# A hybrid encoder layer: gate/up pairs of both FFNs by seven block products, four token quarters, and x kept in DRAM between sub-layers

## The chip, the cores and the metric

One core of one Trainium2 chip runs the whole kernel as one launch. The time is device microseconds of that core, the median of three runs. Five engines work side by side: TensorE (PE, with its weight loads listed apart as PEld), VectorE (DVE), ScalarE (ACT), GpSimd (POOL), and SyncE (SP), which issues most DMAs. Matrix products land in eight PSUM banks; DVE and ACT read them out.

## The reference, cut to what matters

1024 prompt tokens and 32 sample tokens go together through one layer, so every product has 1056 token columns. d_model is 1024 (8 tiles of 128), d_ff 2816 (22 tiles).

```
x += 0.5 * post(SwiGLU_1(pre(x)))            # w_gu 1024x5632, w_down 2816x1024
h = pre(x); z = h @ W_in                     # 8 heads of q|f|i|og, pooling input, gates
yA = up_A(gnorm(HGRN2(q,f,i)) * silu(og));   yB = up_B(pooled mix)
x += post(W_out(sigmoid(gA)*yA + sigmoid(gB)*yB))
x += 0.5 * post(SwiGLU_2(pre(x)))
x += post(sigmoid(pre(x) @ W_pg) * (p @ W_pp))
swiglu(h) = (silu(h @ w_gate) * (h @ w_up)) @ w_down      # pre, post: RMSNorm with gains
```

## The kernel before, in words

Features lie on partitions, tokens on the free axis. The 1056 tokens are G = 3 groups of N = 352. The precision is kept by splitting both operands into two float16 parts, so each 128x128 weight tile costs three matmuls per group (lines 524 to 526: high weight by high x, high weight by low x, low weight by high x).

Weights stream in as units of four tiles (128x512 float32, 256 KB). SP loads a unit into a ring of 11 slots once PE has finished with the slot (line 423). POOL then makes the two float16 parts with three operations: times 32 into `wtmp` (471), high part (473), low part (475), and counts `unit_ready`.

Nothing reorders work at run time: each engine has its own program written by hand, and semaphores tie them. `STAGES` lists the stages: `units` per turn, `turns`, `ks` (how many weight tiles each output column sums over) and `banks`. A turn makes the output tiles (t, g) in order "M" (all groups of column t, then the next), "G" (all columns of group g, then the next) or "P" (pairs), and tile number `pos` of a turn goes to PSUM bank `pos % banks`. PE may start a tile only when the bank's last content was read (`take`, `bank_read`). Every unit of a turn keeps its slot in the next turn, so a turn's units are reloaded as PE leaves them.

- `ffn*_up` computes 44 gate and up columns, 11 turns of 4 columns. ACT applies Silu to a gate tile from PSUM (785), DVE multiplies the up tile in (1170) and splits the product into `hid` (1173, 1174).
- `ffn*_down` sums 22 tiles per column, 2 columns a turn, the last turn in order G. ACT squares (803) and copies (811) each output tile.
- Between sub-layers, per group: `post` scales and adds into x (1133, 1135), `pre` sums squares (1092, 1095), scales (1105) and splits h (1112). These are DVE's; ACT squares (766) and makes the high part (775).
- `heads`: eight turns in which PE computes the next head's four columns and, hooked in between tiles, the pieces of the last head's recurrence (605, 618, 633, 638, 649). DVE frees the q and og tiles by finishing their Silu (1203, 1197).
- `gates`: per output column m, two gate columns (ACT, 984), then the two up-projections, whose tiles DVE multiplies (1409) and joins with three SBUF operations (1415 to 1417).
- `ple`: gate and embedding columns, 2 turns in order G.

Of the kernel before, what the change touches and what calls it, by code (L numbers as in the profile page):

```python
# [13 lines left out]
P = 128  # L22
# [9 lines left out]
G = 3  # L32
N = T // G
C = 64
# [4 lines left out]
UT = 4  # L39
PARTS, PART = 4, KD // 4  # L40

# [5 lines left out]
    "ffn1_up": dict(units=8, turns=11, ks=[KD] * 4, kinds="G" + "P" * 10, banks=6),  # L47
    "ffn1_down": dict(units=11, turns=4, ks=[KF] * 2, kinds="MMMG", banks=6),
    "head0": dict(units=8, turns=1, ks=[KD] * 4, kinds="G", banks=6),
    "heads": dict(units=8, turns=HEADS, ks=[KD] * 4, kinds="M" * HEADS, banks=4),  # L50

    "gates0": dict(units=8, turns=1, ks=[KD, KD, 1, 1, 1, 1, KD, 4], kinds="M", banks=6),
    "gates": dict(units=7, turns=7, ks=[KD, KD, KD, 4], kinds="M" * 7, banks=6),
    "out0": dict(units=6, turns=1, ks=[KD] * 3, kinds="M", banks=3),
    "out1": dict(units=10, turns=1, ks=[KD] * 5, kinds="G", banks=5),
    "ffn2_up": dict(units=8, turns=11, ks=[KD] * 4, kinds="G" + "P" * 10, banks=6),
    "ffn2_down": dict(units=11, turns=4, ks=[KF] * 2, kinds="MMMG", banks=6),
    "ple": dict(units=10, turns=2, ks=[KD, KP] * 4, kinds="GG", banks=6),
}
ORDER = list(STAGES)  # L60
RING = max(s["units"] for s in STAGES.values())
# [12 lines left out]
CALLS += [("post", 3, g) for g in range(G)]  # L74
Y_STAGES = [["ffn1_down"], ["out0", "out1"], ["ffn2_down"], ["ple"]]

# [23 lines left out]

NEXT_UP, NEXT_PLE = 2, 3
# [5 lines left out]


# [11 lines left out]
EARLY = [1, 2, 1]  # L120
# [9 lines left out]
def jobs_of(name, kind):  # L130

    a = len(STAGES[name]["ks"])
    if kind == "M":
        return [(t, g) for t in range(a) for g in range(G)]
    if kind == "G":
        return [(t, g) for g in range(G) for t in range(a)]
    return [(2 * q + r, g) for q in range(a // 2) for g in range(G) for r in range(2)]


class Plan:  # L140


    def __init__(self):
        uses = [0] * 8
        unit = 0
        loads = [0] * RING
        first = 0
        self.base, self.unit0, self.load0, self.first, self.used0 = {}, {}, {}, {}, {}
        used = 0
        self.hg_base = None  # L150
        self.norm = []
        norm_uses = iter(range(len(CALLS)))

        def norms(k):
            for _ in range(k):
                c = next(norm_uses)
                b = 6 + c % 2
                self.norm.append((b, uses[b]))
                uses[b] += 1

        before = {"ffn1_up": 3, "head0": 6, "ffn2_up": 6, "ple": 6}
        for name in ORDER:
# [3 lines left out]
            self.unit0[name] = unit  # L166
# [1434 lines left out]
```

## Time and profile before

| | us |
|---|---|
| median of 3 runs (lowest, highest) | 2683.82 (2682.93, 2685.84) |
| span of the profiled execution | 2682.0 |
| PE busy / PEld busy | 2512.2 / 1654.7 |
| DVE / ACT / POOL busy | 1139.9 / 468.1 / 1528.6 |

The profiled execution's span lies 1.8 us below the median of the runs. PE's busy time is modelled: a matmul is listed at about 0.31 us, while two that follow each other start closer together than that, so the busy share says only where PE stood still. How far a stage is from PE's pace is read from a window's length and its count of matmuls. POOL's idle time before line 471 is nearly all a wait for a weight load, which in turn waits for PE to leave the slot.

### The profile page before, as it was taken

What the parts mean: (1) busy time and instruction counts of PE and PEld (TensorE: products, weight loads), DVE (VectorE), ACT (ScalarE), POOL (GpSimd) and SP (SyncE); (2) the same over time, 40 slices, a digit from 0 to 9 for tenths busy, and PEclk for the clock granted to TensorE, in tenths of its full rate; (3) what the DMA queues carried; (4) which work ended last, traced back from release to release, by engine and by line L of the source; (5) the groups of instructions that cost most, each with busy time, mean ns of one, the idle gap of its engine ahead of it and who ended that gap; (6) DMA issues with size and microseconds to landing.
All of it is one profiled execution on the core that took longest, in us unless ns stands there. A gap on an engine that the chain in (4) does not pass through costs nothing.

```text
span 2682.0 us, 43535 instructions
## 1 busy us (share of the span) xinstructions
PE 2512.2 (94%) x17172; PEld 1654.7 (62%) x17172; DVE 1139.9 (43%) x1526; ACT 468.1 (17%) x782; POOL 1528.6 (57%) x1293
## 2 busy tenths in 40 slices
PE   5999999999979898989899999979999999999797
PEld 3666666666646666666565666646666666666454
DVE  7322222100386677767773233285222222010854
ACT  3000000000222222222220000132000000001243
POOL 4765566766375545454643667744666657565531
PEclk9999999999989999999999999999999999999999
DMA  2211111121011111111110111101111112111111
GB/s 101 64 47 47 47 51 54 52 59 44 24 44 37 35 34 34 34 34 34 47 35 28 44 54 63 44 28 48 47 47 47 47 47 63 56 44 44 56 40 65
DMA packets 74973, 125.28 MB, mean 47 GB/s; under 512 B 9744, under 2 KB 19984, under 8 KB 74896
## 3 DMA queue, kind: packets, MB, share of 16 engines
q1 hardware_dynamic: 66096, 118.26, 14.7%
q10 hardware_dynamic: 8800, 5.94, 0.7%
q8 instruction: 55, 0.90, 0.1%
q14 instruction: 22, 0.18, 0.0%
HBM read 118.73 MB, written 5.44 MB: 46 GB/s over the span
## 4 chain that ended last, share of the span: by engine, by line
PE 77%; DVE 18%; issue 3%; POOL 1%; ACT 1%; DMA 0%; DVEq 0%; POOLq 0%; ACTq 0%
PE bank L524 24%; PE bank L525 24%; PE bank L526 24%; DVE hid L1276 3%; DVE scratch L1105 2%; DVE x L1135 1%; DVE hy L1133 1%; DVE hid L1250 1%; DVE u L1092 1%; DVE part_sum L1092 1%; PE bank L638 1%; DVE hy L1112 1%; PE bank L547 1%; PE bank L618 1%; PE bank L605 1%
## 5 line engine op out<-in xcount | busy, mean ns | idle before, releaser
L524 PE MATMUL bank<-hy,ring 128*128 128x352 f16 x3552 | 1123.9, 316 | 26.2 <-DVE hy L1112 12.5
L525 PE MATMUL bank<-hy,ring 128*128 128x352 f16 x3552 | 1122.4, 316 | 0.0
L526 PE MATMUL bank<-hy,ring 128*128 128x352 f16 x3552 | 1121.5, 316 | 0.0
L471 POOL TENSOR_TENSOR wtmp<-ring,wconst 128x512 f32<-128x512 f32 x429 | 482.6, 1125 | 1032.7 <-DMA ring<-weights 1004.3
L475 POOL TENSOR_TENSOR ring<-wtmp,ring 128x512 f16<-128x512 f32 x429 | 539.8, 1258 | 33.7
L473 POOL TENSOR_TENSOR ring<-wtmp,wconst 128x512 f16<-128x512 f32 x429 | 505.8, 1179 | 33.6
L524 PE MATMUL bank<-hid,ring 128*128 128x352 f16 x1593 | 501.3, 315 | 7.7 <-DVE hid L1397 6.0
L525 PE MATMUL bank<-hid,ring 128*128 128x352 f16 x1593 | 500.9, 314 | 0.0
L526 PE MATMUL bank<-hid,ring 128*128 128x352 f16 x1593 | 500.6, 314 | 0.0
L524 PEld LDWEIGHTS bank<-hy,ring 128*128 128x128 f16 x3552 | 352.1, 99 | 220.3 <-DVE hy L1112 15.9
L526 PEld LDWEIGHTS bank<-hy,ring 128*128 128x128 f16 x3552 | 351.3, 99 | 189.0
L525 PEld LDWEIGHTS bank<-hy,ring 128*128 128x128 f16 x3552 | 351.2, 99 | 186.6 <-issue 3.2
L1170 DVE SCALAR_TENSOR_TENSOR pair_buf<-bank,pair_buf 128x352 f32<-128x352 f32 x132 | 69.2, 524 | 615.2 <-PE bank L526 613.7
L1127 DVE TENSOR_TENSOR u<-u,pair_buf 128x352 f32<-128x352 f32 x84 | 64.8, 771 | 411.3 <-ACT pair_buf L803 410.7
L524 PEld LDWEIGHTS bank<-hid,ring 128*128 128x128 f16 x1593 | 156.9, 98 | 92.8 <-DVE hid L1397 6.4
L525 PEld LDWEIGHTS bank<-hid,ring 128*128 128x128 f16 x1593 | 156.9, 98 | 85.9 <-issue 3.6
L526 PEld LDWEIGHTS bank<-hid,ring 128*128 128x128 f16 x1593 | 156.8, 98 | 83.3
L785 ACT ACTIVATE pair_buf<-bank 128x352 f32<-128x352 f32 x132 | 60.7, 463 | 822.5 <-PE bank L526 822.5
L1174 DVE TENSOR_TENSOR hid<-pair_buf,hid 128x352 f32 (+1 forms) x132 | 124.5, 943 | 17.5
L1409 DVE SCALAR_TENSOR_TENSOR hid<-bank,hid 128x352 f32<-128x352 f32 x48 | 24.9, 519 | 188.1 <-PE bank L526 188.1
L547 PE MATMUL bank<-u,cst 128*128 128x352 f32 x48 | 27.4, 663 | 71.8 <-DVE u L1095 47.1
L1276 DVE TENSOR_TENSOR hid<-hid 128x1088 f32<-128x1088 f32 (+1 forms) x64 | 91.0, 1488 | 0.0
(127 smaller groups left out, 1505.8 us busy)
## 6 DMA issues: line engine op xcount, KB each, us to landing
ring<-weights SPq DMA_DIRECT2D x429, 256.0 KB, 2.6
out_x<-x SPq DMA_DIRECT2D x12, 352.0 KB, 2.3
x<-xT ACTq DMA_DIRECT2D x4, 704.0 KB, 5.9
x<-xT SPq DMA_DIRECT2D x2, 704.0 KB, 5.2
hid<-pT ACTq DMA_DIRECT2D x1, 1056.0 KB, 5.3
out_states<-scratch ACTq DMA_DIRECT2D x16, 64.0 KB, 2.4
scratch<-state_in ACTq DMA_DIRECT2D x8, 64.0 KB, 1.8
cst<-consts ACTq DMA_DIRECT2D x1, 128.0 KB, 5.2
```

Of the source, the lines that this page charges most:

```text
L471: chain.inc(nc.gpsimd.tensor_tensor(wtmp[:], raw, ws_all, ALU.mult))
L473: chain.inc(nc.gpsimd.tensor_tensor(hi, wtmp[:], one_all, ALU.mult))
L475: done.inc(nc.gpsimd.tensor_tensor(lo, wtmp[:], hi, ALU.subtract))
L524: nc.tensor.matmul(out, whi, rhs(t, k, g, 0), start=(k == 0), stop=False)
L525: nc.tensor.matmul(out, whi, rhs(t, k, g, 1), start=False, stop=False)
L526: mm = nc.tensor.matmul(out, wlo, rhs(t, k, g, 0), start=False, stop=end)
L547: nc.tensor.matmul(bank[b][:, 0:N], ones, ssq(g), start=True, stop=True).then_inc(bank_full[b], 1)
L785: nc.scalar.activation(pair_buf[:, n % 2, :], bank[b][:, 0:N], ACT.Silu, scale=1.0 / WS)\
L1127: V_.tensor_tensor(ssq(g), ssq(g), pair_buf[:, n % 2, :], ALU.add).then_inc(ysq_added, 1)
L1170: V_.scalar_tensor_tensor(out=s, in0=bank[b][:, 0:N], scalar=1.0 / WS, in1=s, op0=ALU.mult, op1=ALU.mult).then_inc(bank_read[b], 1)
L1174: V_.tensor_tensor(dst[:, N:2 * N], s, dst[:, 0:N], ALU.subtract).then_inc(hidden_ready, 1)
L1276: V_.tensor_tensor(out, out, in0, ALU.mult).then_inc(operand_ready, 1)
```

## The change

Groups: G = 4, N = 264. PSUM banks per stage: 7 for tiles (banks 0 to 6) and bank 7 for the norms' sums, where 6 and 2 stood (heads keep 4). The ring has 16 slots.

Gate and up tiles j are computed as one 2x2 block product: the two output columns by the two halves of the 8 k-tiles (weight blocks a, b, c, d of one unit each), times the two halves of h by two token quarters. Seven products (Winograd's form, with the u sums taken after PSUM) of 4 k-tiles replace eight. Columns 0 and 1 of gate and up are still computed directly (`up0`, one turn of 4 columns), then 20 pairs follow. The sums of h (T1 to T4) are made once per FFN, before the pairs; those of the weights once per pair.

```diff
-G = 3
+G = 4
+RING = 16
+BANKS = 7
-    "ffn1_up": dict(units=8, turns=11, ks=[KD] * 4, kinds="G" + "P" * 10, banks=6),
-    "ffn1_down": dict(units=11, turns=4, ks=[KF] * 2, kinds="MMMG", banks=6),
+    "ffn1_up0": dict(units=8, turns=1, ks=[KD] * 4, kinds="G", banks=BANKS),
+    "ffn1_up": dict(pairs=KF - 2),
+    "ffn1_down": dict(units=11, turns=4, ks=[KF] * 2, kinds="MMMG", banks=BANKS),
...
-    "gates": dict(units=7, turns=7, ks=[KD, KD, KD, 4], kinds="M" * 7, banks=6),
+    "gates": dict(units=7, turns=7, ks=[KD, KD, KD, 4], kinds="M" * 7, banks=BANKS),
...
+PRODUCTS = 7
+OPERAND = (0, 2, 3, 4, 1, 5, 6)
+PAIR_BANKS = ((0, 1), (2, 3), (6, 7), (4, 5), (0, 1), (4, 5), (2, 3))
...
+            def pair(name, p):
+                pool.wait_ge(scaled, p * RAWS + (sums + 4))
...
+                summed(wtmp[:], c, d, ALU.add)
+                pool.wait_ge(wsum_ready, p * RAWS + (sums + 1))
+                summed(f, wtmp[:], a, ALU.subtract)
+                lo(0)
+                pool.wait_ge(wsum_ready, p * RAWS + (sums + 2))
+                lo(1)
+                summed(c, a, c, ALU.subtract)
+                pool.wait_ge(wsum_ready, p * RAWS + (sums + 3))
+                lo(2)
+                lo(3)
+                lo(4)
+                pool.wait_ge(unit_ready, p * PRODUCTS + (plan.ready0[name] + 2))
+                summed(f, b, f, ALU.subtract)
+                pool.wait_ge(wsum_ready, p * RAWS + (sums + 4))
+                lo(5)
+                lo(6)
...
+            def pair(name, p, ready=None):
+                for k in range(PRODUCTS):
+                    for e in range(2):
...
+                        take(b, uses)
+                        for kk in range(KH):
...
+                with act.Fori(0, STAGES[name]["pairs"] - 1) as i:
+                    scale(name, i + 1)
+                    to_high(name, i + 1, range(5), product_before(i))
+                    silu_pair(f, i, 0)
+                    to_high(name, i + 1, [5], product_before(i))
+                    silu_pair(f, i, 1)
+                    to_high(name, i + 1, [6], product_before(i))
...
-                    V_.tensor_tensor(xg(g)[:, ks, :], xg(g)[:, ks, :], y[:, ks, :], ALU.add).then_inc(x_updated, 1)
+                    V_.tensor_tensor(xq(min(q + 1, 3), g)[:, ks, :], xq(min(q + 1, 3), g)[:, ks, :], y[:, ks, :], ALU.add).then_inc(x_updated, 1)
```

So POOL does 11 operations per pair (4 sums, `summed`, and 7 low parts, `lo`) where 12 stood for the same four units; the scaling and the high parts go to ACT (11 operations of 128x512). The weight parts of product k are single: they are remade once product k of the pair before is done. DVE adds each of a pair's 14 PSUM tiles to running sums (`tile`, 128x264 from PSUM), and at the end of a pair does per half a multiplication, a high part and a low part of 128x528. x is no longer resident: ACT's queue stores each quarter to `out_x` after `post` and loads it back during the next down stage (8 stores and 12 loads of 1056 KB).

Four places where the order changed, each as it stands in the programs.

TensorE, the gates stage, from the last two tiles of a turn into the next turn. Before: `hid` as operand is an up-projection tile, `hy` a gate tile of the next turn.

```order
L524 MATMUL bank4<-hid,ring 128x352 [waits bank_read4]
...
L524 MATMUL bank5<-hid,ring 128x352 [waits bank_read5]
...
L518 ISA [waits bank_read0]
L524 MATMUL bank0<-hy,ring 128x352 [waits unit_ready]
...
L524 MATMUL bank1<-hy,ring 128x352 [waits bank_read1]
```

After, the same place:

```order
L714 MATMUL bank0<-hid,ring 128x264 [waits bank_read0]
...
L714 MATMUL bank1<-hid,ring 128x264 [waits bank_read1]
...
L708 ISA [waits bank_read0]
L714 MATMUL bank0<-ops,ring 128x264 [waits unit_ready]
...
L714 MATMUL bank1<-ops,ring 128x264 [waits bank_read1]
```

The first two tiles of a turn now use the banks of the last two tiles of the turn before; before, they used those of its first two up-projection tiles.

VectorE, between the last `pre` and the first pair of an FFN, after: L1507 to L1513 finish a direct tile, L1523 forms a T sum of h, L1533 its low part.

```order
L1507 SCALAR_TENSOR_TENSOR work<-bank4,work 128x264 [waits bank_full4,bank_read3]
...
L1523 TENSOR_TENSOR hid<-hid 128x4x264
L1523 TENSOR_TENSOR hid<-hid 128x4x264 [waits t_summed]
...
L1533 TENSOR_TENSOR ops<-hid,ops 128x4x264 [waits t_hi] x2
L1523 TENSOR_TENSOR hid<-hid 128x4x264 x2
L1507 SCALAR_TENSOR_TENSOR work<-bank6,work 128x264 [waits bank_full6,bank_read5]
...
L1507 SCALAR_TENSOR_TENSOR work<-bank1,work 128x264 [waits bank_full1,bank_read0]
...
L1533 TENSOR_TENSOR ops<-hid,ops 128x4x264 [waits t_hi] x4
```

The direct tiles in banks 0 and 1 are read behind six T sums and two low parts, and the first pair's first product needs those banks.

GpSimd, one pair, after (L636 is a sum, L632 a low part; the operations of before are the three of lines 471, 473 and 475, four times).

```order
L636 TENSOR_TENSOR ring<-wtmp,ring 128x512 [waits wsum_ready]
L627 REGISTER_ALU
L632 TENSOR_TENSOR ring<-ring 128x512 [waits whi_ready]
L653 REGISTER_ALU
L627 REGISTER_ALU [waits wsum_ready]
L632 TENSOR_TENSOR ring<-ring 128x512 [waits whi_ready]
L636 TENSOR_TENSOR ring<-ring 128x512
```

POOL now waits on ACT (`whi_ready`) ahead of each low part, where its three operations of a unit waited only on POOL itself.

## Rows read from the trace of the kernel before

**Rows 1.** Page: busy microseconds, share of the span, instructions.
```profile
PE 2512.2 (94%) x17172; PEld 1654.7 (62%) x17172; DVE 1139.9 (43%) x1526; ACT 468.1 (17%) x782; POOL 1528.6 (57%) x1293
```
**Rows 2.** Windows by stage: from:to length, busy (count) per engine, granted clock, DMA.
```profile
82.10:511.70 429.60, 429.60 (x2882) 281.80 (x2880) 112.36 (x180) 27.79 (x60) 282.72 (x256) 1.00 0.18 51
511.70:762.60 250.90, 242.41 (x1594) 157.52 (x1592) 56.29 (x52) 35.60 (x64) 141.50 (x125) 0.99 0.16 47
827.20:1382.50 555.30, 502.36 (x3986) 351.58 (x3985) 396.04 (x597) 152.47 (x219) 296.61 (x208) 0.96 0.12 35
1434.80:1697.90 263.10, 263.10 (x1766) 172.60 (x1764) 78.30 (x103) 18.80 (x42) 168.54 (x152) 1.00 0.17 52
```
**Rows 3.** Groups by line, weight loads: count, busy us, mean ns, idle before.
```profile
L524 PEld LDWEIGHTS bank<-hy,ring 128*128 128x128 f16 x3552 | 352.1, 99 | 220.3 <-DVE hy L1112 15.9 <-ACT hid L1018 6.3 <-POOL ring L475 5.6
```
**Rows 4.** Chain of waits in a head turn, 34 short f32 products: start, us.
```profile
931.24 2.24 PE bank L605 x68
```
**Rows 5.** Timeline, POOL in the gates stage: start, us, [idle before].
```profile
1446.89 1.04 POOL L471 TENSOR_TENSOR wtmp<-ring,wconst 128x512 f32<-128x512 f32 x1 [31.61 <-DMA ring<-weights]
1448.01 1.04 POOL L473 TENSOR_TENSOR ring<-wtmp,wconst 128x512 f16<-128x512 f32 x1
1449.13 1.15 POOL L475 TENSOR_TENSOR ring<-wtmp,ring 128x512 f16<-128x512 f32 x1
...
1472.96 1.20 POOL L473 TENSOR_TENSOR ring<-wtmp,wconst 128x512 f16<-128x512 f32 x1
1474.24 1.32 POOL L475 TENSOR_TENSOR ring<-wtmp,ring 128x512 f16<-128x512 f32 x1
```
**Rows 6.** Timeline, PE in the gates stage.
```profile
1443.61 0.31 PE L526 MATMUL bank<-hy,ring 128*128 128x352 f16 x1
...
1467.03 0.31 PE L524 MATMUL bank<-hid,ring 128*128 128x352 f16 x1
```
**Rows 7.** Timeline, DVE over the joins of that turn.
```profile
1469.09 0.52 DVE L1409 SCALAR_TENSOR_TENSOR hid<-bank,hid 128x352 f32<-128x352 f32 x1 [1.27 <-PE bank L526]
...
1473.18 0.51 DVE L1409 SCALAR_TENSOR_TENSOR hid<-bank,hid 128x352 f32<-128x352 f32 x1
...
1476.98 0.51 DVE L1409 SCALAR_TENSOR_TENSOR hid<-bank,hid 128x352 f32<-128x352 f32 x1
```
**Rows 8.** Groups by line and shape, ACT and DVE.
```profile
L1170 DVE SCALAR_TENSOR_TENSOR pair_buf<-bank,pair_buf 128x352 f32<-128x352 f32 x132 | 69.2, 524 | 615.2 <-PE bank L526 613.7 <-ACT pair_buf L785 1.5
L803 ACT ACTIVATE pair_buf<-bank 128x352 f32<-128x352 f32 x63 | 29.0, 460 | 330.1 <-PE bank L526 329.4 <-DVE u L1127 0.7
L811 ACT ACTIVATE hy<-bank,col 128x352 f32<-128x352 f32 x72 | 39.5, 549 | 0.0
L766 ACT ACTIVATE scratch<-x 128x1408 f32<-128x1408 f32 x24 | 32.7, 1375 | 64.5 <-DVE x L1135 59.4 <-issue 5.1
L1272 DVE TENSOR_TENSOR hid<-hid 128x1056 f32 x6 | 7.5, 1258 | 0.9
L1276 DVE TENSOR_TENSOR hid<-hid 128x1088 f32<-128x1088 f32 x32 | 53.4, 1707 | 0.0
```
**Rows 9.** The same view of POOL, 827.2 to 1382.5 us.
```profile
L473 POOL TENSOR_TENSOR ring<-wtmp,wconst 128x512 f16<-128x512 f32 x69 | 102.9, 1491 | 5.4
```
**Rows 10.** Timeline of a head turn, PE, state updates of the last head.
```profile
937.09 2.82 PE L618 MATMUL bank<-hid 64*128 64x128 f32 x32
942.18 0.48 PE L618 MATMUL bank<-hid 64*128 64x128 f32 x2
```
**Rows 11.** The same turn, DVE.
```profile
945.74 1.39 DVE L1203 SCALAR_TENSOR_TENSOR hid<-bank,hid 128x352 f32<-128x352 f32 x3
```
**Rows 12.** Timeline, DVE, last `pre` at the start.
```profile
50.63 2.63 DVE L1092 TENSOR_REDUCE u<-scratch 128x352 f32<-128x1408 f32 x1 [0.47 <-ACT scratch L766]
...
64.78 1.83 DVE L1112 TENSOR_TENSOR hy<-scratch,hy 128x704 f16<-128x704 f32 x2
```
**Rows 13.** Waits of PE, 2590 to 2640 us (`ple`): total, times, longest.
```profile
PE bank L524 <- POOL ring L475: 6.2, 4, 1.7
```

More of the change, by code:

```diff
@@ L181, in __init__, with per @@
                     uses[b] += HEADS * len(HG_PIECES) // 4
-        norms(3)
-        self.units = unit
+        norms(G)
+    def per(self, name, b):
+        s = STAGES[name]
+        return len(range(b, len(s["ks"]) * G, s["banks"]))
     def head_job(self, h, t, g):
@@ L443, in _ @@
                                      name == ORDER[0] and i == 0)
-                for u in range(s["units"]):
-                    last[plan.slot(name, u)] = plan.freed_by(name, s["turns"] - 1, u)
+                last.update(plan.slots_freed(name))
             for g in range(G):
@@ L477, in _ @@
             for name in ORDER:
                 s = STAGES[name]
-                first = 1 if name == ORDER[0] else 0
-                for i in range(first):
-                    for u in range(s["units"]):
-                        split(name, i, u)
-                if s["turns"] - first >= 3:
-                    with pool.Fori(first, s["turns"]) as i:
-                        chain.enter(i, first, 2 * s["units"])
-                        done.enter(i, first, s["units"])
+                if "pairs" in s:
+                    pair(name, 0)
+                    with pool.Fori(1, s["pairs"]) as p:
+                        pair(name, p)
+                    done.base += PRODUCTS * s["pairs"]
+                    continue
@@ L491, in _ @@
                 else:
-                    for i in range(first, s["turns"]):
+                    for i in range(s["turns"]):
                         for u in range(s["units"]):
@@ L1144, in add, with between @@
                         add_square(q, m, g)
+                def between(g):
+                    if g < G - 1:
+                        add(last[g + 1][:early[g + 1]])
+                    if q == 1 and g == 2:
+                        products(1, (0,))
+                    if q == 1 and g == G - 1:
+                        products(1, (2, 3))
+                    if q == 2 and g in (1, 2):
+                        split_p(g - 1)
+                    if q == 2 and g == G - 1:
+                        gated_products(range(NEXT_PLE))
@@ L1157, in products @@
-            def products(name, f, i, kind, ns):
-                pairs = [(pos, t, g) for pos, (t, g) in enumerate(jobs_of(name, kind)) if t % 2]
+                    add(last[g][early[g]:])
+                    if q == 1 and g == G - 1:
+                        products(1, (1,))
+                    c = post_call(q, g)
+                    post(q, c, g, yq(q, g))
+                    dve.wait_ge(x_updated, count_before(UPDATE_PARTS, q, g) + UPDATE_PARTS[q])
+                    pre(q + 1, c + 1, g, lambda: between(g))
```

700 lines of the change are left out of this document (505 added, 195 removed).

## The prediction

> **What bounds the kernel now.** I read the page first, then the windows by stage, then timelines. PE stands still for only 6% of the span [rows 1], and a window of gate/up columns shows why: 2880 f16 matmuls of 352 columns in 429.60 us, 149.2 ns each, at granted clock 1.00 (2.4 GHz) [rows 2]. 352 columns at 2.4 GHz are 146.7 ns, so 2.5 ns come on top. The gates run at the same pace, 1764 in 263.10 us. There PE alone sets the time, POOL is busy for 282.72 of 429.60 us and DVE for 112.36, and fewer columns are worth their full time. It is otherwise in the head turns: 2304 matmuls would need 343.7 us and the window is 555.30. In all, 15,444 f16 matmuls need 2304 of 2682.0 us; the other 378 are recurrence pieces, seams between sub-layers and the start. The question is which of PE's new bank and weight waits end last.
>
> **Matmuls.** At N = 264 a matmul should take 110 + 2.5 = 112.5 ns. Gate and up: before 2 x 3168 of 149.2 ns = 945.3 us. After, per FFN, 384 direct ones and 20 pairs x 7 x 2 x 4 x 3 = 3360; 7488 x 112.5 ns = 842.4 us. That is 103 us less. The other 9108 become 12,144, 1366 us for 1359: 7 us more. The weight load per matmul stays and has less to hide under: 99 ns [rows 3] against 112.5. I take no cost: in the heads, 68 short f32 products, each with its own load, pass in 2.24 us [rows 4], 33 ns each, so loads can follow each other closer than that.
>
> The Trainium skill (TensorE: Matmul & The Clock Gate, Back-to-back issue gap) gives for streams with a load per matmul about 131 ns at 512 columns and 81 ns at 128. The row of 149.2 ns at 352 already contradicts that curve and fits the page's other formula, N/2.4 + 2.5. By the curve's slope (0.13 ns a column) the 88 columns saved would give only 11.5 ns.
>
> **A pair, 18.9 us on PE (168 x 112.5 ns).** Who feeds it?
> - DVE: 14 tiles from PSUM. A PSUM read of 352 takes 524 ns also in the pair loop [rows 8]; less 88 columns at 0.96 per ns, 0.43 us each, 6.0. Then six SBUF operations of 528, 0.44 to 0.71 alone (1056 take 1.26 [rows 8]), at most 1.2 to 1.5 beside POOL. 14 us: under PE.
> - ACT: 1375 ns for 1408 and 460 for 352 [rows 8] give 0.60 us for 512, 13 operations, 8 us.
> - POOL: alone, 1.04, 1.04 and 1.15 us with gaps of 0.08 [rows 5]. A low part is as before, 1.15. A sum reads two full float32 tensors, not shown; between 1.04 and 1.2 I take 1.15, the nearest two-tensor row. 11 x 1.15 + 0.7 of gaps = 13.35. Two low parts start only after a sum and ACT's high part of it, 2 x 0.8 = 1.6. And each pair has a hole: block d may be reloaded only when the last low part is done, and the next pair's first sum needs it scaled. From PE's last use of a unit (1443.61 + 0.31 [rows 6]) to POOL's first operation on its successor (1446.89 [rows 5]) go 3.0 us; plus ACT's 0.6 and a semaphore, 3.7. Sum 18.65.
> - Contention: where DVE runs its joins, POOL's 1.04 becomes 1.20 and 1.15 becomes 1.32 [rows 5], behind DVE operations of 352. Those of 528 hold longer by 0.18 us, so about 0.35 each; three of the six should meet POOL: 1.05. Ends: 0 and, by POOL's 1.49 in the heads [rows 9] on all 11, 3.6. POOL's round is then 19.7 us (18.2 to 22.3), longer than PE's 18.9. POOL sets the pace.
>
> **Entry into the pairs.** Let t be the moment the last quarter of h is split. PE then has 8.8 us of direct tiles (3.25 of the quarter's four tiles at 2.7) and wants banks 0 and 1. Those hold the last two direct tiles, and DVE reaches bank 1 behind two finished tiles, six T sums and two T low parts (the order above). ACT scales four units (2.4), loads its Silu table (1.3), so DVE's two tiles end at t + 7.8; four T sums of 1.26 [rows 8] to 12.9; two low parts to 15.4; two sums beside POOL, 1.7 [rows 8], to 18.9; ACT's T high parts and one weight part (waiting for POOL's third sum) to 20.8, two Silus to 21.6, and bank 1 is free at 23.5. PE waits 13 us. The rest of pair 0 ends at t + 42, one POOL round after its last low part (t + 37.8) is too early for pair 1, whose first weights come at t + 37.8 + 3.7 + 3.6 = t + 45. The last pair ends at t + 45 + 18 x 19.7 + 18.9 = t + 418.5.
>
> t at the start is 66.5 now (end of the last low part [rows 12]). A group costs DVE 13.4 us alone (reductions 2.63 and 2.54, add 0.53, eight of 0.53, four of 0.88); a quarter 10.6. Four for three, one more norm wait (2), two more finished tiles in the chain (2.7), less 2 for the earlier first quarter: t = 71. FFN 1 then ends at 489.5, not 511.7: **-22**. FFN 2 counts from the end of its direct columns, t + 8.8; without the first FFN's sigmoid, 408.7 for 429.6: **-21**. Without POOL's pace and the entry this would be -52 each.
>
> **Down stages.** With POOL one round behind, it is done with the last pair 7 us before PE, two units' worth. The first tile wants six units in 7.4 us where POOL makes one in 3.46 [rows 5]: wait 7.5, some of it repaid in a slow clock, 9. Eight tiles on seven banks also put a turn's last tile and the next turn's first in bank 0: PE waits for ACT's square and copy (0.39 + 0.47 from 460 and 549 ns [rows 8], plus latency), 1.2 us x 3. In the last turn one quarter passes all 11 units in 14.9 us instead of 19.7, 2.4 more. 15 a stage: **+30**.
>
> **Head turns, +16.** The first f tile now uses the bank of the first q tile, which DVE frees after the state chain. In the row, updates start on PE at 937.09 [rows 10] and DVE's q multiplications at 945.74 [rows 11], first one done at 946.2: 9.1 us. PE's way from there to that f tile is now 2.8 (updates) + 0.5 + 33 matmuls (3.7), 7.0. The difference of 2.2 and latency, 2.3, seven turns. Before, that bank was free anyway.
>
> **Gates, +38.** The last up-projection tiles of a turn take PE 1.35 us each, and DVE joins one per 4.1 and 3.8 us (1469.09, 1473.18, 1476.98 [rows 7]): each of three SBUF operations waits for a POOL operation, so the smaller size saves little, 3.6. Counted from the first such matmul (1467.03 [rows 6]), the reads come at 1.6, 5.2, 8.8 and 12.4. The next turn's first gate tile needs bank 0, that is the third read: PE arrives at 5.4, gets it at 9.3, and the second tile waits from 12.0 to 12.9. 4.8 us x 7 = 33.6, and 4.4 for clock lost after such pauses. Were DVE alone, 2.0 a tile, it would be 0.7 x 7 = 5; with every pause slowing the clock, 46.
>
> **Seams and ends.** Quarters start the seam sooner (-4) and end it sooner (-3.5); DVE pays four sets of fixed costs (+5) and at the second seam two more tiles; I take -1 for three seams, bounds -20 and +25. `ple`'s second turn wants ten units in 13.5 us instead of 17.9; it waits 6.2 us for POOL now [rows 13], +8. The last post is shorter, -3. The DRAM copies of x are asked for a whole down stage ahead and stay hidden; uncovered, each would cost some 5 us, once per quarter.
>
> **Sum against the profiled span:** -22 - 21 + 30 + 16 + 38 - 1 + 8 - 3 + 7 = +52, minus 1 for what the stage sums already hold of the last 7 = +51: 2733, and with the 1.8 us to the median 2735.
>
> **Rivals.**
> 1. *DVE and POOL seldom meet* (faster). The six operations fall into POOL's hole, POOL's round is 18.2 and PE's 18.9 decides; the lead grows 0.7 per pair, so the down stages find their units. Each FFN -14 and -9, and joins at 2.0 a tile, -33: 2735 - 46 - 33 = 2656. It decides from contention under 0.25 us per pair. For it: the tail of a pair starts when POOL has 2 us left to do. Against: joins were slowed in every gates turn. 0.20.
> 2. *Only the bank waits fail to appear* in gates and heads, because DVE is earlier than I place it: 2735 - 54 = 2681, no change. Against: both orders are fixed. 0.09.
> 3. *POOL is slower:* a round of 21.5, as towards the heads' rows; 18 x 1.8 x 2 = +65: 2800. 0.14.
> 4. *Matmul spacing does not shrink with N:* the slope above gives 137.7 ns, 25.2 x 19,632 = +495. The pace of 33 ns [rows 4] speaks against it. 0.02.
>
> **Numbers.** Forecast 2735, chance 0.55, own range 2700 to 2770. For 8 in 10 the range goes to the first rival and most of the third: 2652 to 2795. A change under 0.2% (5.4 us) is what a measurement cannot tell from none. Faster 0.22 (rival 1 and a part of 2), same 0.05, slower 0.73.
>
> **What would show it.** A pair at 19 to 20 us between the starts of its first products, with PE waiting for POOL ahead of them; near 18.9 and no wait: rival 1. An idle PE of 13 us ahead of each first pair. 4 us ahead of the first gate tile of each gates turn, released by DVE's multiplication. 2 us ahead of the first f tile. Matmul starts 112 to 113 ns apart. The prediction is wrong if a pair takes under 18.9 or if those four waits sum to less than half of what is set down.

## The result, and the profile after

| | us |
|---|---|
| changed kernel, median of 4 runs (lowest, highest) | 2764.86 (2762.32, 2767.49) |
| kernel before, 4 runs beside it | 2684.11 (2682.93, 2685.84) |
| ratio, 95% interval | 1.0302 (1.0285 to 1.0318) |
| span of the profiled execution after | 2760.5 |

It became slower by 81 us, where +51 was forecast. The time lies inside the range, the sign is right, and the size is too small by 30 us. Both spans (2760.5 and 2682.0) differ by 78.5 us, and that difference can be laid out by stage from the start times of the matmuls:

| stretch | before | after | difference | forecast |
|---|---|---|---|---|
| start to the end of FFN1's pairs | 511.7 | 487.4 | -24.3 | -22 |
| `ffn1_down`, `head0` | 315.5 | 341.5 | +26 | +15 and a share of the seams' -1 |
| head turns | 555.3 | 594.1 | +39 | +16 |
| `gates0` | 52.3 | 43.8 | -8.5 | 0 |
| `gates`, `out0` | 295.3 | 338.6 | +43 | +38 |
| `out1` to the end of FFN2's pairs | 552.8 | 529.0 | -24 | -21 |
| `ffn2_down`, `ple`, tail | 399.0 | 426.2 | +27 | +15 and +5 |

The forecast column leaves out the +6 that its sum had for matmuls outside the FFNs (7, less 1), since no single stretch holds them. The profiled executions themselves scatter: in experiments that do not touch the heads, the head turns took 589 to 599 us, so a difference of a few microseconds in that row is not to be read.

The windows of after for the four stretches of [rows 2], same columns:

```profile
93.60:487.40 393.80, 384.46 (x3361) 328.69 (x3362) 254.36 (x407) 146.54 (x257) 285.62 (x224) 0.99 0.20 58
487.40:760.50 273.10, 245.39 (x2124) 208.96 (x2121) 74.15 (x80) 41.35 (x89) 168.57 (x150) 0.98 0.24 74
828.90:1423.00 594.10, 518.69 (x4755) 433.08 (x4753) 398.22 (x611) 157.31 (x251) 297.07 (x213) 0.93 0.12 34
1466.80:1770.20 303.40, 275.59 (x2354) 233.97 (x2351) 92.78 (x140) 21.85 (x56) 175.50 (x161) 0.96 0.18 50
```

The first is the pair stage alone (20 pairs). Its length over 3360 matmuls is 117 ns each at clock 0.99; the median spacing of two starts is 113 ns. In the fourth PE is busy 275.59 of 303.40 us, where it had no pause before.

The waits of PE over the whole span, after (engine, buffer and line that waited, releaser: total, times, longest):

```profile
PE bank L760 <- DVE u L1451: 46.1, 7, 12.1
PE bank L714 <- POOL ring L619: 28.5, 17, 2.7
PE bank L714 <- DVE hid L1831: 27.8, 8, 4.2
PE bank L760 <- DVE u L1419: 24.6, 5, 12.4
...
PE bank L745 <- ACT work L1009: 21.9, 2, 11.5
PE bank L745 <- DVE work L1550: 16.3, 31, 3.0
```

L760 is the norms' sum, L714 a direct tile, L745 a tile of a pair. The third row is the gates' bank wait of the forecast (24.3 us of it in `gates`), the fifth of those shown is the entry into the two FFNs' pairs (13 forecast for each, 11.5 and 10.4 came), the last the pace of the pairs. The second row is weight units, 7.8 us in the first down stage, 7.9 in the second and 12.9 in `ple`, about what was set down. The waits for the norms' sums, the first and the fourth row, are large but not new. Together they are 70.7 us, and before they were 71.8:

```profile
PE bank L547 <- DVE u L1095: 47.1, 10, 14.4
PE bank L547 <- DVE u L1127: 24.7, 4, 10.5
```

What is new between the end of FFN1 and the end of `head0`, beside the units and the bank hand-overs, are two waits of `head0` tiles for banks that ACT and DVE have still to read (waits of PE, 660 to 830 us; no tile waited so there before):

```profile
PE bank L714 <- ACT hid L1171: 9.4, 1, 9.4
PE bank L714 <- DVE hid L1617: 8.6, 1, 8.6
```

POOL in one pair, after, timeline (start, us, operation, [idle before <- releaser]); L636 is a sum, L632 a low part:

```profile
268.95 1.27 POOL L636 TENSOR_TENSOR wtmp<-ring 128x512 f32<-128x512 f32 x1 [3.76 <-ACT ring L1016]
270.30 1.27 POOL L636 TENSOR_TENSOR ring<-wtmp,ring 128x512 f32<-128x512 f32 x1
...
275.76 1.16 POOL L632 TENSOR_TENSOR ring<-ring 128x512 f16<-128x512 f32 x1 [0.74 <-ACT ring L1030]
...
277.99 1.63 POOL L632 TENSOR_TENSOR ring<-ring 128x512 f16<-128x512 f32 x1
279.57 1.46 POOL L636 TENSOR_TENSOR ring<-ring 128x512 f32<-128x512 f32 x1
281.77 2.74 POOL L632 TENSOR_TENSOR ring<-ring 128x512 f16<-128x512 f32 x2 [0.74 <-ACT ring L1030]
288.26 1.27 POOL L636 TENSOR_TENSOR wtmp<-ring 128x512 f32<-128x512 f32 x1 [3.75 <-ACT ring L1016]
```

From one first sum to the next is 19.31 us. The pairs of PE are as long: 25.0 and 21.0 us for the first two, then 19.2 to 19.4 (the last one 19.9 and 19.8). PE does not wait for POOL's operand though, but for DVE's copy out of bank 0. The way there is through two engines' fixed orders:

```profile
281.06 0.63 ACT L1030 ACTIVATE ring<-ring 128x512 f16<-128x512 f32 x1 [3.81 <-POOL ring L636]
281.60 0.63 ACT L1037 ACTIVATE work<-work 128x528 f32<-128x528 f32 x1
```

```profile
282.26 1.24 DVE L1578 SCALAR_TENSOR_TENSOR work<-work 128x528 f32<-128x528 f32 x1 [0.66 <-ACT work L1037]
283.64 1.16 DVE L1580 TENSOR_SCALAR hid<-work 128x528 f32 x1
284.94 0.71 DVE L1581 TENSOR_TENSOR hid<-work,hid 128x528 f32 x1
285.57 0.77 DVE L1550 COPY work<-bank 128x264 f32<-128x264 f32 x2
```

POOL's fourth sum (279.57) lets ACT make the high part (L1030), behind which the Silu stands (L1037), behind which DVE's tail of the old pair stands, behind which the copy that frees the bank stands (L1550). Whether POOL's round or this order sets the pace the trace alone does not tell; e3 and e5 do.

DVE in the gates, the joins of one turn, after:

```profile
1500.77 0.43 DVE L1831 SCALAR_TENSOR_TENSOR hid<-bank,hid 128x264 f32<-128x264 f32 x1 [0.99 <-PE bank L716]
...
1503.90 0.42 DVE L1831 SCALAR_TENSOR_TENSOR hid<-bank,hid 128x264 f32<-128x264 f32 x1
...
1507.51 0.42 DVE L1831 SCALAR_TENSOR_TENSOR hid<-bank,hid 128x264 f32<-128x264 f32 x1
...
1511.12 0.42 DVE L1831 SCALAR_TENSOR_TENSOR hid<-bank,hid 128x264 f32<-128x264 f32 x1
```

and PE there:

```profile
1508.06 0.28 PE L714 MATMUL bank<-ops,ring 128*128 128x264 f16 x1 [3.35 <-DVE hid L1831]
1511.59 0.29 PE L714 MATMUL bank<-ops,ring 128*128 128x264 f16 x1 [0.66 <-DVE hid L1831]
```

The joins come every 3.1 to 3.6 us (4.1 and 3.8 in [rows 7]), and the two gate tiles wait for the third and the fourth.

### The profile page after: what moved, and what is told of

Its sections match the earlier page's. It is cut to its first block, busy times and chain, and to the rows that moved or that the text cites. A ratio compares the mean times of both kernels' runs of the same rounds, so it can differ in the third digit from the quotient of the medians.

```text
span 2760.5 us, 54906 instructions
## 1 busy us (share of the span) xinstructions
PE 2460.6 (89%) x21376; PEld 2078.2 (75%) x21376; DVE 1478.1 (54%) x2188; ACT 760.0 (28%) x1378; POOL 1537.5 (56%) x1253
## 4 chain that ended last, share of the span: by engine, by line
PE 42%; POOL 20%; DVE 19%; issue 10%; DMA 4%; ACT 3%; POOLq 1%; DVEq 0%; ACTq 0%; SPq 0%
PE bank L714 13%; PE bank L715 13%; PE bank L716 13%; POOL ring L632 10%; POOL ring L636 4%; DMA ring<-weights 4%; DVE hid L1696 2%; POOL wtmp L636 2%; DVE work L1749 2%; DVE work L1429 1%; POOL wtmp L615 1%; POOL ring L617 1%; DVE hid L1429 1%; POOL ring L619 1%; ACT ring L1016 1%
## 5 line engine op out<-in xcount | busy, mean ns | idle before, releaser
L615 POOL TENSOR_TENSOR wtmp<-ring,wconst 128x512 f32<-128x512 f32 x269 | 302.4, 1124 | 799.3 <-DMA ring<-weights 779.7
L714 PE MATMUL bank<-ops,ring 128*128 128x264 f16 x2176 | 624.1, 287 | 88.0 <-DVE hid L1831 24.3
L745 PE MATMUL bank<-ops,ring 128*128 128x264 f16 x2240 | 621.2, 277 | 40.2 <-ACT work L1009 21.9
L714 PE MATMUL bank<-hid,ring 128*128 128x264 f16 x2124 | 593.6, 279 | 36.1 <-POOL ring L619 17.8
L715 PE MATMUL bank<-ops,ring 128*128 128x264 f16 x2176 | 623.4, 286 | 0.0
L716 PE MATMUL bank<-ops,ring 128*128 128x264 f16 x2176 | 622.3, 286 | 0.0
L747 PE MATMUL bank<-ops,ring 128*128 128x264 f16 x2240 | 620.9, 277 | 0.0
L748 PE MATMUL bank<-ops,ring 128*128 128x264 f16 x2240 | 620.8, 277 | 0.0
L715 PE MATMUL bank<-hid,ring 128*128 128x264 f16 x2124 | 593.2, 279 | 0.0
L716 PE MATMUL bank<-hid,ring 128*128 128x264 f16 x2124 | 592.9, 279 | 0.0
L632 POOL TENSOR_TENSOR ring<-ring 128x512 f16<-128x512 f32 x240 | 315.9, 1330 | 85.2 <-ACT ring L1030 85.2
L619 POOL TENSOR_TENSOR ring<-wtmp,ring 128x512 f16<-128x512 f32 x269 | 346.5, 1288 | 21.1
L617 POOL TENSOR_TENSOR ring<-wtmp,wconst 128x512 f16<-128x512 f32 x269 | 318.2, 1183 | 21.1
L714 PEld LDWEIGHTS bank<-ops,ring 128*128 128x128 f16 x2176 | 221.6, 102 | 140.3 <-POOL ring L619 31.8
L1451 DVE TENSOR_TENSOR u<-u,work 128x264 f32<-128x264 f32 x112 | 69.3, 618 | 417.6 <-ACT work L1087 416.7
L745 PEld LDWEIGHTS bank<-ops,ring 128*128 128x128 f16 x2240 | 220.0, 98 | 85.5 <-issue 23.5
L714 PEld LDWEIGHTS bank<-hid,ring 128*128 128x128 f16 x2124 | 210.4, 99 | 75.7 <-POOL ring L619 13.9
L716 PEld LDWEIGHTS bank<-ops,ring 128*128 128x128 f16 x2176 | 221.0, 102 | 40.6
L715 PEld LDWEIGHTS bank<-ops,ring 128*128 128x128 f16 x2176 | 220.7, 101 | 40.5 <-issue 0.6
L748 PEld LDWEIGHTS bank<-ops,ring 128*128 128x128 f16 x2240 | 220.1, 98 | 33.8
L747 PEld LDWEIGHTS bank<-ops,ring 128*128 128x128 f16 x2240 | 220.1, 98 | 33.1
L1030 ACT ACTIVATE ring<-ring 128x512 f16<-128x512 f32 x240 | 148.8, 621 | 342.4 <-POOL ring L636 342.2
```

What stands on the lines that cost most here:

```text
L615: chain.inc(nc.gpsimd.tensor_tensor(wtmp[:], raw(slot), ws_all, ALU.mult))
L617: chain.inc(nc.gpsimd.tensor_tensor(high(slot), wtmp[:], one_all, ALU.mult))
L619: done.inc(nc.gpsimd.tensor_tensor(low(slot), wtmp[:], high(slot), ALU.subtract))
L632: nc.gpsimd.tensor_tensor(low(slot), weight_source(name, k), high(slot), ALU.subtract)\
L714: nc.tensor.matmul(out, whi, rhs(t, k, g, 0), start=(k == 0), stop=False)
L715: nc.tensor.matmul(out, whi, rhs(t, k, g, 1), start=False, stop=False)
```

## The experiments

All were timed beside the kernel before on the same chip; "gain" is against the changed kernel's 2764.9 us (the kernel before stood at 2684 to 2686 us each time). Their intervals are about ±4 us (±7 for e6 and e12, ±5 for e5 and e11, ±2.5 for e8 and e9).

**e1, six banks in the downs and gates.**

```diff
-    "ffn1_down": dict(..., banks=BANKS),
+    "ffn1_down": dict(..., banks=6),
-    "gates": dict(..., banks=BANKS),
+    "gates": dict(..., banks=6),
-    "ffn2_down": dict(..., banks=BANKS),
+    "ffn2_down": dict(..., banks=6),
```

> The changed kernel with tiles of both down stages and of the gates stage in six banks (0 to 5) where it uses seven. Theory (the bank hand-over is what the gates stage lost): the first gate tile of a turn no longer uses the bank of an up-projection tile that is still to be joined, the gates window falls from 303.5 us to about 265 to 270 (the window of before was 263.1), and the one-microsecond hand-overs of the down turns go: 35 to 45 us faster than the changed kernel in all. Rival (the joins of quarters are slower than PE's tiles in any bank): the wait moves to the second or third gate tile and the window falls by less than 15 us.

Measured 2717.3 us, ratio 1.0128 (1.0113 to 1.0144): 47.5 us gained, a little above what was expected. The gates window:

```profile
1462.40:1727.00 264.60, 264.60 (x2354) 230.14 (x2353) 90.25 (x136) 20.50 (x56) 165.88 (x152) 1.00 0.19 57
```

2352 matmuls of 112.5 ns are 264.6 us, so nothing is left of the loss. 38.9 us come from here, 2.0 from `out0`, 6.4 from the two downs. Of the 38.9, 27.8 were PE's idle time in that window (24.3 of it listed as this wait); the rest is PE's busy time, which was 11.0 us longer at a granted clock of 0.96 against 1.00.

**e2, the first q tile of a head turn ahead of the state chain.** DVE finishes it before the chain instead of after.

```diff
+                if not u_turn:
+                    silu_q(h, 0, 1 + G)
...
-                    for g in range(G):
+                    for g in range(1, G):
```

> The changed kernel with the first q tile of a head turn finished by DVE ahead of the state chain. Theory (the first f tile waits for that read): the wait of 2.3 us per turn ahead of the first f tile goes, 14 to 25 us faster with the clock that it costs. Rival (the turn is bound by the state chain on DVE): the wait comes back at a later f or og tile, under 5 us gained.

Measured 2738.4 us, ratio 1.0194 (1.0180 to 1.0208): 26.5 us gained, above the 14 to 25 expected. The head window, and the wait that is gone from it (after's row):

```profile
831.00:1394.80 563.80, 506.42 (x4755) 429.03 (x4753) 397.49 (x611) 157.24 (x251) 296.58 (x213) 0.95 0.13 36
```

```profile
PE bank L714 <- DVE hid L1623: 14.1, 7, 2.1
```

The wait was 2.0 us per turn (2.3 forecast), but its removal gave 30 us in this window. PE's idle time fell by 18.0 us, of which 14.1 are this wait and the rest others of the same turns that became a little shorter, and its busy time fell by another 12.3 us, at a granted clock of 0.95 where 0.93 stood.

**e3, the second Silu of a pair ahead of the POOL-bound high part.**

```diff
-                    to_high(name, i + 1, [5], product_before(i))
                     silu_pair(f, i, 1)
+                    to_high(name, i + 1, [5], product_before(i))
```

> The changed kernel with ACT's second Silu of a pair moved ahead of the high part of weight product 5. Theory (POOL's round of 19.3 us sets the pair's pace): pairs stay at 19.2 to 19.4 us and only the entry gains, under 8 us in all. Rival (the Silu that stands behind a POOL-bound high part sets it, through DVE's tail and the copy of product 0 from bank 0): PE's wait of 0.5 us in each pair goes, pairs take 18.9 us, 16 to 22 us faster in both FFNs together.

Measured 2765.3 us, ratio 1.0306 (1.0289 to 1.0322): no gain. Pairs stayed at 19.2 to 19.5 us. The chain through ACT and DVE that stands above is only the way in which POOL's pace reaches PE; the rival falls.

**e4, the last direct tiles ahead of the T sums.**

```diff
-                silus(f, (4, 5))
+                silus(f, (4, 5, 6, 7))
...
-                silus(f, (6, 7))
```
(and `products` on DVE in the same way)

> The changed kernel with the last direct tiles of each FFN finished by ACT and DVE ahead of the T sums of h. Theory (PE's stop of 11 us ahead of the first pair is first the bank, then the T sums and weight parts behind it): the wait for bank 0 goes and a wait for the T parts and the first weight parts stands in its place; 4 to 8 us gained per FFN, 8 to 16 in all. Rival (POOL's round is what the pairs start from anyway): the stop ahead of pair 0 shrinks and the one ahead of pair 1 grows by the same amount, no gain.

Measured 2767.8 us, ratio 1.0321 (1.0304 to 1.0338): no gain. The stop ahead of pair 0 went from 11.5 to 9.8 us and is now ended by POOL's weight part (L632) instead of ACT's Silu; inside pair 0 a stop of 3.0 us became 4.5, and pair 0 took 27.7 us instead of 25.0. So the bank is not what sets the entry. That leaves the T sums and weight parts, which no run made shorter.

**e5, one weight sum of a pair over one of its 512 columns.** That product is then not that of the block formula.

```diff
-                summed(c, a, c, ALU.subtract)
+                summed(c[:, 0:1], a[:, 0:1], c[:, 0:1], ALU.subtract)
```

> The changed kernel with the third weight sum of each pair made over one column of 512 (its product is then not that of the block formula): POOL's round of a pair loses some 1.2 us and nothing else changes. Theory (POOL's round of 19.3 us sets the pair's pace): pairs fall to PE's own 18.9 us, 14 to 18 us over both FFNs, and as POOL then gains a lead on PE, the 6 us that the first down tile waits for its units go as well: 22 to 30 us faster than the changed kernel. Rival (DVE's copy of product 0 is late through DVE's own work, and the 0.3 us belong to it): pairs stay above 19.2 us and under 8 us are gained, all in the down stages.

Measured 2734.0 us, ratio 1.0184 (1.0166 to 1.0202): 30.9 us gained. From the third on every pair takes 18.90 us, PE's own 168 x 112.5 ns. The FFN windows gain 8.5 and 8.3 us, the downs 5.8 and 7.8. The shortened sum took 0.19 us instead of 1.27. So 1.1 us less on POOL took PE's wait away from the third pair on: POOL's round sets the pace.

**e6, the copies of x at an eighth of their size.** Only k-tile 0 is stored and loaded back.

> The changed kernel with the stores of x to DRAM and its loads back at an eighth of their size (one of eight k-tiles; x is then wrong in the rest). Theory (the copies lie beside a whole down stage and cost nothing): within 4 us of the changed kernel. Rival (they take DMA time from the weight loads, or DVE waits for x at each post): 8 to 30 us faster, in the down stages and seams.

```diff
-                    act.dma_start(out_x[:, :, xcols(g)], xq(p, g)).then_inc(x_saved[g], 16)
+                    act.dma_start(out_x[:, 0:1, xcols(g)], xq(p, g)[:, 0:1, :]).then_inc(x_saved[g], 16)
```
(the loads in the same way)

Measured 2770.3 us, ratio 1.0312 (1.0287 to 1.0338), 5 us above the changed kernel with overlapping intervals: the copies are hidden.

**e7, the reductions in `pre` over one k-tile of four.** The norms are then of a part of the features.

```diff
-... hq(p, g)[:, ks, :].rearrange(
+... hq(p, g)[:, ks, :][:, 0:1, :].rearrange(
```

> The changed kernel with the two reductions of each quarter's squares in `pre` made over one k-tile of four (the norms are then of a part of the features): each falls from about 1.95 us to some 0.6. Theory (DVE's chain of post and pre sets the end of a seam between sub-layers, so a microsecond of DVE there is a microsecond of the kernel): 8 reductions x 1.3 = 10 us per seam, and less at the start, where ACT's squares lead: 25 to 40 us faster in all. Rival (PE's tiles, behind its own waits for banks and norms, set it): under 10 us.

Measured 2762.3 us, ratio 1.0284 (1.0268 to 1.0299): 2.6 us gained where I expected 25 to 40. Each reduction did fall from 1.99 to 0.43 us:

```profile
L1416 DVE TENSOR_REDUCE u<-work 128x264 f32<-128x264 f32 x4 | 1.7, 428 | 0.1
```

In the seam of FFN1 DVE had 12 us less to do, and yet from the end of FFN1 to the end of `head0` it took 342.5 us, against 341.5 in the changed kernel. DVE stood idle longer instead, for the norms' sums and for ACT's squares. My theory that DVE's work alone is the seam's bound fell. At the start, ahead of FFN1's pairs, less work on DVE did help: PE's wait for the norms' sums there fell from 18.0 to 12.5 us, and the first pair began at 88.0 us instead of 93.6. That gain of 5.6 us is hidden in the total by the head turns, which took 599.1 us in this profiled execution for 594.1, within their scatter.

**e8, e1 and e2 together.**

> The two edits that gained, together: six tile banks in both down stages and the gates, and the first q tile of a head turn finished ahead of the state chain. The gains were 47 and 26 us in different stages. Theory (they are independent): 2688 to 2696 us, about 0.2 to 0.4% slower than the kernel before. Rival (part of the one was clock won back that the other wins as well): 2696 to 2710.

Measured 2685.0 us (11 runs), ratio 0.9998 (0.9989 to 1.0007). That is 80 us against the changed kernel, where the two gains sum to 74: 3 us below the range I had set, but within what the intervals of the three allow. The two gains are independent, and with them the changed kernel stands level with the kernel before. More than what the products win (67 us, e12) had been lost in places that hold no product.

**e9, the norm sums where their inputs are ready.** On top of e8; each pair is (tile, k).

```diff
-            down("ffn1_down", 0, {(2, 5): calls(4), (3, 15): calls(5), (4, 5): calls(6), (6, 3): calls(7), (6, 6): calls(8)})
-            turn("head0", ..., {(0, 6): calls(9), (1, 0): calls(10), (7, 4): calls(11)})
+            down("ffn1_down", 0, {(2, 2): calls(4), (4, 1): calls(5), (5, 4): calls(6), (6, 15): calls(7), (7, 20): calls(8)})
+            turn("head0", ..., {(0, 3): calls(9), (1, 0): calls(10), (7, 4): calls(11)})
```
(`ffn2_down` and `ple` in the same way)

> The combination of e8, with PE's norm sums of both down stages and of what follows put where their inputs are ready. In e8's trace PE issues the sum for the second quarter's `pre` 5.0 us after DVE has it (728.9 and 734.0) and the third's 4.9 us after (757.4 and 762.3), and in `ple` the last 8 us after, while it stands 3.6, 4.4 and 10.3 us at others that come too soon. Theory (the seam is a chain that runs back and forth between DVE's rounds and these hooks, so lateness of PE counts in full, and less work on DVE alone counts for nothing): about 10 us less in each of the two, 15 to 25 us in all. Rival (PE's own tiles and its seven banks bound the seam, as e7 suggests too): under 5 us.

Measured 2677.7 us, ratio 0.9970 (0.9961 to 0.9980): 7.3 us against e8, under what the theory wanted and over the rival. Down and `head0` together gained 2.1 us, `ffn2_down` and `ple` 4.0. The sum for the second quarter's `pre` came 3.2 us earlier (730.8 for 734.0), and then DVE took twice as long over that `pre`. DVE in e8:

```profile
735.43 1.70 DVE L1429 SCALAR_TENSOR_TENSOR work<-ops,col,rinv 128x264 f32<-128x264 f32 x4 [6.48 <-ACT rinv L975]
737.05 1.54 DVE L1436 TENSOR_TENSOR ops<-work,ops 128x528 f16<-128x528 f32 x1
...
742.43 1.50 DVE L1436 TENSOR_TENSOR ops<-work,ops 128x528 f16<-128x528 f32 x2
```

and in e9:

```profile
732.28 4.88 DVE L1427 SCALAR_TENSOR_TENSOR work<-ops,col,rinv 128x264 f32<-128x264 f32 x4 [1.75 <-ACT rinv L973]
737.08 1.54 DVE L1434 TENSOR_TENSOR ops<-work,ops 128x528 f16<-128x528 f32 x1
...
744.98 3.11 DVE L1434 TENSOR_TENSOR ops<-work,ops 128x528 f16<-128x528 f32 x2
```

POOL's busy time from 730 to 750 us, in e8 and in e9 (windows; the fifth busy time is POOL's):

```profile
730.00:750.00 20.00, 11.05 (x74) 8.39 (x73) 12.08 (x16) 5.92 (x11) 3.90 (x3) 0.74 0.28 83
```

```profile
730.00:750.00 20.00, 10.98 (x92) 9.20 (x91) 17.54 (x15) 4.23 (x8) 16.70 (x14) 0.87 0.61 192
```

PE, held up less, frees ring slots earlier, POOL splits the next stage's units just while DVE does its `pre`, and each DVE operation of 264 takes 1.22 us instead of 0.43. A part of the gain on PE is paid back on DVE.

**e10, the fourth weight sum on DVE.** On top of e8, with nothing left out.

```diff
+            def weight_sum(f, p):
+                dve.wait_ge(wsum_ready, p * RAWS + (plan.sum0[name] + 3))
+                dve.wait_ge(unit_ready, p * PRODUCTS + (plan.ready0[name] + 2))
+                V_.tensor_tensor(wf, wb, wf, ALU.subtract).then_inc(wsum_ready, 1)
...
                     V_.tensor_tensor(c1(e)[:, 0:N], src, s1(e), ALU.add).then_inc(read, 1)
+                if following:
+                    weight_sum(f, p + 1)
```

> The combination of e8, with the fourth weight sum of each pair (of pairs 1 to 19) moved from POOL to DVE, behind the two tiles of product 4. The sums are the same. Theory (POOL's round sets the pair, and DVE has about 5 us to spare of 18.9): POOL's round goes to about 18.0, pairs to 18.9 to 19.0, and the first down tile finds its units: 25 to 32 us faster than e8, as in e5. Rival (DVE's added operation delays its tail and the copy of product 0, or meets POOL, so that the wait stays with another releaser): under 12 us.

Measured 2655.8 us, ratio 0.9889 (0.9875 to 0.9904): 29.3 us against e8. Pairs take 18.90 us. DVE's tail even became shorter, since it now falls into a stretch in which POOL works less. Its first operation over 19 pairs, in after and in e10 (count, busy us, mean ns, idle before):

```profile
L1578 DVE SCALAR_TENSOR_TENSOR work<-work 128x528 f32<-128x528 f32 x38 | 48.3, 1271 | 46.7 <-ACT work L1037 46.7
```

```profile
L1589 DVE SCALAR_TENSOR_TENSOR work<-work 128x528 f32<-128x528 f32 x38 | 32.2, 847 | 0.2
L1542 DVE TENSOR_TENSOR ring<-ring 128x512 f32<-128x512 f32 x19 | 24.3, 1280 | 16.3 <-POOL ring L636 16.3
```

**e11, e9 and e10 together.**

> Both edits of e9 and e10 together. Theory (different stretches, independent but for the first down turn): the sum of the two gains within 4 us, 2635 to 2650 us. Rival (POOL's lag and PE's early hooks hide each other): 5 to 10 us less than the sum.

Measured 2645.1 us, ratio 0.9855 (0.9836 to 0.9874). The gains of 7.3 and 29.3 add up (39.9 against e8). This version beats the kernel before by 40 us, 1.45%.

**e12, the changed kernel without block products.** Ten further direct turns of four columns; quarters, banks, ring and copies as changed.

```diff
-    "ffn1_up": dict(pairs=KF - 2),
+    "ffn1_up": dict(units=8, turns=10, ks=[KD] * 4, kinds="P" * 10, banks=BANKS),
```

> The changed kernel without the block products: all 44 gate and up columns computed directly, in ten further turns of four columns in pair order as before, but in four quarters, with seven tile banks, sixteen ring slots and the copies of x to DRAM. So against the kernel before it shows what the rest of the change costs, against the changed kernel what the seven products bring. Theory (the products bring back 48 us in the two FFN windows and give some 12 us of that back in unit waits of the first down tiles and at the entry; everything outside the FFNs is lost to quarters and banks): start to the end of FFN1 at 510 to 518 us where 487.4 stood, first down tile without unit waits, 2795 to 2810 us in all, 4.1 to 4.7% slower than before. Rival (direct tiles of quarters lose time too, through a clock that falls or readers that come late, so that the products' worth is more than 48): over 2815 us.

Measured 2831.6 us, ratio 1.0544 (1.0518 to 1.0570). That is in the rival's range, but not by its mechanism, since the direct tiles of quarters lost no time: the block products are worth 67 us, not 48 less 12, and the rest of the change costs 147. The direct turns themselves take 432.0 us for 3840 matmuls, exactly 112.5 ns, in both FFNs, against 393.8 and 393.3 for the pairs: 38.2 and 38.7 us. The downs found their units and were 5.1 and 7.1 us shorter, as the theory had it. But FFN1 ended at 527.7 us, not before 518: I had expected the 11.5 us of entry to go, and the first turn of the stage ended at 95.7 us all the same, where the pairs began at 93.6. The last `pre` ends at 86.1 us here and at 72.3 in the changed kernel. The time is lost in the second and the third quarter's `pre`. In the second the same DVE operations take, here

```profile
40.28 4.91 DVE L1398 SCALAR_TENSOR_TENSOR hid<-hid,col,rinv 128x264 f32<-128x264 f32 x4 [2.31 <-ACT rinv L972]
```

and in the changed kernel

```profile
39.86 1.71 DVE L1429 SCALAR_TENSOR_TENSOR hid<-hid,col,rinv 128x264 f32<-128x264 f32 x4 [2.31 <-ACT rinv L975]
```

POOL is busy 27.99 of the 30 us from 30 to 60 us here, splitting the second turn's units into the large ring, and 6.75 in the changed kernel, where from 37 to 75 us it waits for blocks scaled by ACT. That is the same mechanism as in e9.

## Why the prediction was right, and where it was short

- **Matmul spacing.** 112.5 ns forecast, median 113 in the changed kernel and 112.5 in stretches without a pause (e1, e5, e12). The loads hid. The row that I took this from did not show it: its loads are of 64 columns [rows 4], half as wide as these. With 149.2 ns at 352 columns [rows 2] that is N/2.4 + 2.5 twice. The curve of the Trainium skill (TensorE: Matmul & The Clock Gate, Back-to-back issue gap), by whose slope from the row at 352 columns 137.7 ns would have stood here, is contradicted a second time.
- **A pair, 19.7 us set by POOL.** 19.3 came. POOL was the cause, shown by e5 and e10, with e3 against the rival. Within the sum, POOL's two-tensor float32 operations took 1.27 us where I had 1.15, so the eleven are 13.2 us without contention for 12.65. The hole was 3.76 for 3.7, the two waits for ACT 1.5 for 1.6, and contention 1.1 for 1.05 (low parts of 1.63 and 1.37 us beside others of 1.16, a sum of 1.46). What did not come is the 0.7 us of gaps: listed operations overlap by 0.3 us instead. The range's lower end was wrong on its own terms, which give 18.65 without contention and not 18.2. I expected PE to be seen waiting for POOL; it waited for DVE's bank copy, through orders I had not followed. Whoever reads only PE's releaser would blame DVE.
- **Entry.** t = 71 forecast, 72.3 came; the wait 13 against 11.5; the second pair at t + 45 against t + 46.4 (118.7). The FFNs, -22 and -21, became -24.3 and -23.7, by the smaller round. e4 shows that it is not the bank; that it is the T sums and weight parts is what remains, not shown by a run of its own.
- **Gates, +38.** The window alone is +40.3 and e1 returned 38.9 of it. Place and tiles were as forecast; the listed waits were shorter (24.3 us for 33.6) and the clock dearer (11.0 for 4.4), so the near hit is two errors that offset.
- **Heads, +16: the first term that was mis-sized.** The wait at the first f tile was found at the place and nearly at the length forecast (2.0 us for 2.3), but the sum took its length for its price. e2 measured 26 to 30 us, 3.8 to 4.3 us per turn, double. In the gates I had added 4.4 us of clock for pauses; in the heads I added nothing. Of the remaining 8.5 us in the head window (563.8 against 555.3), 4.1 are the wait for ACT at the end of the head turns (L864), 7.9 us for 3.8. `gates0` is 8.5 us shorter, which I had not foreseen: PE waited 6.0 us there before and does not now, and its busy time is 2.5 us less at a granted clock of 0.99 for 0.92. I take the one wait to have moved to the other, which no run shows.
- **Down stages and seams, +30 and -1: the second term that was mis-sized.** The two stretches with a down came out at +26 and +27, not +15 each. Unit waits (6.0 us at the first down tile against 7.5 forecast) and bank hand-overs (1.0 us each against 1.2) were in the sum and are right. What was missing in the last down turn is PE's stops for the norms' sums, 4.05, 5.66 and 10.27 us from matmul to matmul, where 4.90 and 6.88 stood before. In `head0` two such stops of before went (waits of 9.7 and 4.5 us), and in their place PE waits 9.4 and 8.6 us for banks, which ACT and DVE read only behind their share of the last quarter. I read this as a seam that runs late by DVE's and ACT's rounds, whichever instruction of PE meets it. What failed is the step that a quarter's smaller operations save on DVE what the fourth set of fixed costs adds. DVE's groups in that seam, before (713.2 to 805.3 us) and after (695.8 to 801.5), the scaling in `pre`:

```profile
L1105 DVE SCALAR_TENSOR_TENSOR scratch<-x,col,rinv 128x352 f32<-128x352 f32 x24 | 18.9, 839 | 6.7 <-ACT rinv L755 6.7
```

```profile
L1429 DVE SCALAR_TENSOR_TENSOR work<-ops,col,rinv 128x264 f32<-128x264 f32 x32 | 23.3, 776 | 12.2 <-ACT rinv L975 12.2
```

A third more operations, each only 8% shorter for 25% fewer elements, since POOL splits beside them. I had divided durations by size from operations that ran alone. e7 shows that even this is not the whole: in this seam, taking work off DVE alone gave nothing. My reading is that the round runs DVE, ACT, PE's norm sum and back, with PE's sums at fixed places. e9 moved those and got 7.3 of an expected 15 to 25 us. How the loss of a seam divides between DVE's longer rounds, PE's places and POOL's contention stays open.
- **`ple` +8, tail -3.** The waits for units came (12.9 us in 7, against the 6.2 us of [rows 13]), so the +8 was nearly right, yet `ple` and the tail together were only 0.5 us longer than before. PE's waits for the norms' sums were 1.6 us in this stretch, where they had been 12.2: they had moved ahead, into the last down turn, and the forecast had no term for that. Together the two terms were too large by some 5 us.
- **Copies of x, hidden.** e6 agrees.

That the time lies inside the range owes something to luck: the heads, the down stretches and the gates came out 47 us above their terms, and `gates0`, the FFNs and the 6 us of other matmuls 20 us below.

Rival 1 (2656) is not what happened in the changed kernel, yet its price was real: e5 and e10 made POOL's round shorter than PE's by an edit, which is what its condition would have done, and got 31 and 29 us of its 46, and e1 got more than its 33 for the joins by another way.

## What to carry to other kernels

When a tile size shrinks, follow every PSUM bank and every fixed place in another engine's order that was matched to the old size; here two small edits in stages that hold no block product were worth 80 us, as much as the whole loss. Price a pause of PE that comes once per turn above its length. Here a microsecond of idle PE cost 1.4 us in the gates (38.9 for 27.8) and 1.7 in the heads (30.3 for 18.0), since PE's busy time was longer too, at a lower granted clock. A wait's releaser is the last link; take away a little work on each engine of the loop, one at a time, to find which one sets the pace.

## What the runs showed of the hardware

- A matmul of 264 columns with its own weight load of 128x128 float16 follows the last one after 112.5 ns, over 3840 of them without a pause.
- DVE and POOL slow each other when both read and write float32 in SBUF, and DVE suffers more: 1.22 us against 0.43 for a 128x264 operation, 1.55 against 0.75 for 128x528 into float16 (e9, e8). DVE's operations with an operand in PSUM stayed at 0.42 to 0.43 us throughout the pairs and the gates. One-input operations suffer too: the one of L1838 takes 0.91 us against 0.30 in the gates. POOL's own rise less, from 1.04 to 1.12 us in e9 and from 1.16 to at most 1.63 in a pair. The Trainium skill (SBUF — State Buffer, SBUF: two separate sides) has this as a port pair that one of the two locks for a whole instruction when DVE has two inputs in SBUF, or is in a 2-port mode, against a POOL operation that reads SBUF. The traces agree for two inputs: 1.22 us is nearly the 1.12 of the POOL operation that each waits for.
- So an engine can lose by another's head start. POOL, splitting early, delayed the last `pre` of the start by 14 us in e12, and in e9 a norm sum that came 3.2 us earlier led to a `pre` that ended 4.2 us later.
- POOL's operation on two full float32 tensors of 128x512 takes 1.27 us, against 1.04 with one of them broadcast [rows 5].
